# Attention of the first block: values of four heads as one feature-major product, masks on VectorE, copies on ScalarE

## What is computed

```python
def block(i):                       # 128 queries t; 8 heads of 64 in two key groups of four
    s_c = einsum("bqgrd,bkgd->bgrqk", qb, k_cmp) * scale
    p_c = masked_softmax(s_c, cmp_end[None, :] <= t[:, None])
    o_c = einsum("bgrqk,bkgd->bqgrd", p_c, v_cmp)
    ...
    s_s = einsum("bqgrd,bgqkd->bgrqk", qb, ks) * scale
    p_s = masked_softmax(s_s, causal)
    o_s = einsum("bgrqk,bgqkd->bqgrd", p_s, vs)
    ...
    s_w = einsum("bqgrd,bkgd->bgrqk", qb, kw) * scale
    p_w = masked_softmax(s_w, mask_w)
    o_w = einsum("bgrqk,bkgd->bqgrd", p_w, vw)
    o = gb[..., 0:1] * o_c + gb[..., 1:2] * o_s + gb[..., 2:3] * o_w
...
mixed = concatenate([rmsnorm(y_conv, norm_conv_out), rmsnorm(y_att, norm_attn_out)])
h = h + rmsnorm(mixed @ w_out, norm_mix_post)
mn = rmsnorm(mem, norm_mem)         # memory rows for the cross attention that follows
```

## Time and profile before

| | |
|---|---|
| median of 3 runs | 2248.43 us (2248.36 to 2249.26) |
| profiled execution, span from first to last instruction | 2246.4 us |
| its own time | not given beside the span; the median is 2.0 us above the span |
| PE busy | 2224.9 us, 99% |
| DVE, ACT, POOL busy | 1245.1 us (55%), 885.6 us (39%), 280.7 us (12%) |
| chain that ended last | PE 93%, DVE 3%, POOL 1%, ACT 1% |
| DMA | 203.19 MB, mean 90 GB/s |

### The profile page before, as it was taken

The page is one execution under the profiler, slowest core; times in us unless marked ns, Lnnn a source line. Parts: engine busy times, 40 slices in busy tenths (PEclk is TensorE's granted clock), DMA queues, the critical chain, the costliest instruction groups (busy, mean ns, idle before and its releaser), DMA issues.

```text
span 2246.4 us, 29245 instructions
## 1 busy us (share of the span) xinstructions
PE 2224.9 (99%) x11388; PEld 1821.7 (81%) x11388; DVE 1245.1 (55%) x1836; ACT 885.6 (39%) x1363; POOL 280.7 (12%) x273
## 2 busy tenths in 40 slices
PE   9999999999999999999999999999999999999999
PEld 7877888898888888886778888888887668888887
DVE  6467656445444225999664444333889664544422
ACT  5545454354333225234744333222323753433321
POOL 3000032011000001014331000001003442000000
PEclk9999999999999999999999999999999999999999
DMA  6221033122222231321122222222221112322222
GB/s 223 100 76 57 20 121 126 55 72 99 103 102 93 94 113 69 113 75 57 56 77 81 107 93 93 100 106 105 104 84 57 39 66 85 113 102 104 94 101 86
DMA packets 30484, 203.19 MB, mean 90 GB/s; under 512 B 3504, under 2 KB 4144, under 8 KB 6704
## 3 DMA queue, kind: packets, MB, share of 16 engines
q1 hardware_dynamic: 29088, 197.34, 24.4%
q10 hardware_dynamic: 1296, 4.46, 0.5%
HBM read 199.69 MB, written 2.10 MB: 90 GB/s over the span
## 4 chain that ended last, share of the span: by engine, by line
PE 93%; DVE 3%; POOL 1%; ACT 1%; issue 1%; DMA 0%; ACTq 0%; DVEq 0%; POOLq 0%
PE bank L415 26%; PE bank L417 26%; PE bank L416 26%; PE bank L2110 1%; PE bank L1002 1%; PE bank L2120 1%; PE bank L2133 1%; PE bank L973 1%; PE bank L2028 1%; POOL acc L324 1%; PE bank L990 1%; PE bank L2010 1%; PE bank L1593 1%; PE bank L1570 1%; PE bank L515 1%
## 5 line engine op out<-in xcount | busy, mean ns | idle before, releaser
L415 PE MATMUL bank<-x_hi,w_hi 128*128 128x512 f32 (+1 forms) x2032 | 789.9, 389 | 5.9 <-DVE x_lo L1766 2.3
L417 PE MATMUL bank<-x_hi,w_lo 128*128 128x512 f32 (+1 forms) x2032 | 775.0, 381 | 0.0
L416 PE MATMUL bank<-x_lo,w_hi 128*128 128x512 f32 (+1 forms) x2032 | 774.1, 381 | 0.0
L301 DVE TENSOR_TENSOR w_lo<-w_raw,w_hi 128x2048 fp32r<-128x2048 f32 x167 | 386.2, 2313 | 412.3 <-ACT w_hi L297 412.3
L297 ACT ACTIVATE w_hi<-w_raw 128x2048 fp32r<-128x2048 f32 x167 | 319.7, 1916 | 585.8 <-PE bank L417 583.9
L415 PEld LDWEIGHTS bank<-x_hi,w_hi 128*128 128x128 f32 x2032 | 382.1, 188 | 83.6 <-issue 6.8
L417 PEld LDWEIGHTS bank<-x_hi,w_lo 128*128 128x128 f32 x2032 | 381.9, 188 | 74.9
L416 PEld LDWEIGHTS bank<-x_lo,w_hi 128*128 128x128 f32 x2032 | 382.4, 188 | 72.7 <-issue 2.9
L415 PE MATMUL bank<-f_hi,w_hi 128*128 128x512 f32 (+1 forms) x572 | 213.3, 373 | 0.0
L416 PE MATMUL bank<-f_lo,w_hi 128*128 128x512 f32 (+1 forms) x572 | 213.2, 373 | 0.0
L417 PE MATMUL bank<-f_hi,w_lo 128*128 128x512 f32 (+1 forms) x572 | 213.2, 373 | 0.0
(11 more groups left out here) (355 smaller groups left out, 2637.2 us busy)
## 6 DMA issues: line engine op xcount, KB each, us to landing
w_raw<-w_d SPq DMA_DIRECT2D x184, 1024.0 KB, 4.8
out_d<-h SPq DMA_DIRECT2D x8, 256.0 KB, 6.6
h<-x_d ACTq DMA_DIRECT2D x3, 512.0 KB, 9.2
tab<-rope_d ACTq DMA_DIRECT2D x2, 640.0 KB, 3.9
memT<-mem_d ACTq DMA_DIRECT2D x1, 1024.0 KB, 4.8
w_raw<-w_d SPq DMA_DIRECT2D x2, 256.0 KB, 4.1
h<-x_d ACTq DMA_DIRECT2D x2, 256.0 KB, 5.8
w_raw<-w_d SPq DMA_DIRECT2D x1, 512.0 KB, 6.6
```

Source lines behind the costliest of these rows:

```text
L301: dve.tensor_tensor(w_lo[:, u.slot, :], w_raw[:, u.slot, :], w_hi[:, u.slot, :], ALU.subtract).then_inc(lo_ready, 1)
L415: pe.matmul(dst, wh[:, k, cols], hi[:, kx_, at:at + width], start=start, stop=False)
L416: pe.matmul(dst, wh[:, k, cols], lo[:, kx_, at:at + width], start=False, stop=False)
L417: return pe.matmul(dst, wl[:, k, cols], hi[:, kx_, at:at + width], start=False, stop=stop)
```

## The change

- A job's pair of heads is now one head of each key group (m and m + 4), so `kTx` goes; the columns of the query weights and gates and the rows of the output weights are reordered on the host. Jobs 0 to 3 of a block are the selected branch, 4 to 7 the window.
- The mask products go. DVE subtracts and masks out of PSUM into `prob` and takes the minimum in one instruction per head (`minima`); the exponential then works in place. `prob` has four buffers, so scores wait for the minimum and no longer for the exponential.
- POOL multiplies each job's probabilities by gate over sum (`job_scaled`) before they are turned; DVE does so for the compressed branch.
- The turn comes three steps after the scores; ACT copies all turned probabilities, four jobs side by side into `pT`.
- The values of four jobs are one run of products, four steps behind the last of them: 64 value columns are the weights, 512 columns (four jobs) move, and each head half writes its 64 partitions of bank 6. Both branches sum up there, and DVE adds the sum to `o_all`, now feature-major, once per block (`block_out`).
- The attention norm follows the new layout: squares summed on POOL and PE, the inverse root spread to a row, four multiplications on DVE; `mixed_turn` goes.
- The tables of the steps move, four partial output tiles (`TAIL_TILES`) stand among the last turns, and the last products and the memory rows' sums are in another order.

The core of the diff (of replaced functions the new lines; the old ones stand in the listing above):

```diff
+        J_LAG_T, J_LAG_V, C_LAG_T, C_LAG_V = 3, 4, 2, 3
+        J_STEPS = JOBS + J_LAG_V
+        J_VALUES_AT = {js[-1] + J_LAG_V: n for n, js in enumerate(J_GROUPS)}
+
+        def block_end(b_):
+
+            return 8 * b_ + 7 + J_LAG_V
...
+        GATED_AT = {**{t: 3 for t in range(-QB, 0)}, **{t: 4 for t in range(8)}, **{t: 2 for t in range(8, 16)}}
...
+        SPLIT_AT = {0: (14, 0), 1: (14, 1), 9: (15, 0), 10: (15, 1), 14: (16, 0), 15: (16, 1), 18: (17, 0), 20: (17, 1)}
+
+        CONV_AT = {6: 0, 7: 2, 8: 4, 11: 6, 12: 8, 13: 10, 16: 12, 17: 14}
+        CONV_SQ_AT = {8: (0,), 12: (1,), 14: (2,), 18: (3,)}
+        AT_CONV_SUM, AT_CONV_INV, AT_CONV_ROWS = 20, 21, 26
+        CONV_NORM_AT = {26: (0, 1), 27: (2, 3)}
+        CONV_HI_AT = {27: (0, 1), 28: (2, 3)}
+        CONV_LO_AT = {28: (0, 1), 29: (2, 3)}
+        MEM_EARLY = 2
...
-            return j // 8, j % 8 // 2, j % 2, j % 8 // 4
+            return j // 8, j % 4, j % 8 // 4
...
             def c_turn(i):
-                pe.wait_ge(j_exp, i + 1)
+                pe.wait_ge(c_w, 4 * i + 4)
...
+                for m in range(4):
+                    for e in range(2):
+                        mm = pe.matmul(bank[HD * e:HD * e + HD, 6, m * P:(m + 1) * P], vblk[:, e, m * HD:(m + 1) * HD],
+                                       pt_c[:, i % 2, e * P:(e + 1) * P], start=True, stop=True)
...
                 else:
-                    pe.wait_ge(j_exp, QB + 2 * (j - 1))
+                    pe.wait_ge(j_max, QB + 2 * (j - 1))
                 for e in range(2):
                     pe.matmul(bank[:, b_ + e, 0:n], qT[HD * e:HD * e + HD, m, i * P:(i + 1) * P],
-                              key_rows(kT, kTx, e, g)[:, br, 0:n], start=True, stop=False)
-                for e in range(2):
-                    mm = pe.matmul(bank[:, b_ + e, i * P:n], ident_b[:, :], mask_b[:, P:2 * P], start=False, stop=True)
-                mm.then_inc(j_s, 1)
+                              kT[HD * e:HD * e + HD, br, 0:n], start=True, stop=True).then_inc(j_s, 1)
...
             def turn(j):
                 i = j // 8
-                pe.wait_ge(j_exp, QB + 2 * (j + 1))
+                pe.wait_ge(j_scaled, j + 1)
                 pe.wait_ge(j_pta, QB + j)
...
+            def values(n):
+                js = J_GROUPS[n]
+                i, m0, br = job(js[0])
+                m1 = m0 + len(js)
+                pe.wait_ge(j_pta, QB + js[-1] + 1)
+                if br == 0:
+                    pe.wait_ge(j_o, QB + i)
+                for k in range(i + 1):
+                    for e in range(2):
+                        mm = pe.matmul(bank[HD * e:HD * e + HD, 6, m0 * P:m1 * P], vtok[:, k, br * P + e * HD:br * P + (e + 1) * HD],
+                                       pT[:, k, e, m0:m1, :].rearrange("p m t -> p (m t)"),
+                                       start=(br == 0 and k == 0), stop=(br == 1 and k == i))
                 mm.then_inc(j_pv, 1)
...
+            TAIL_TILES = {JOBS: (0, 0), JOBS + 1: (0, 1), JOBS + 2: (1, 0), JOBS + 3: (1, 1)}
+            for t in range(-QB, J_STEPS):
                 if t < 0:
                     c_scores(t + QB)
                 elif t < JOBS:
                     scores(t)
+                if 0 <= t + QB - C_LAG_V < QB:
+                    c_values(t + QB - C_LAG_V)
+                if t in J_VALUES_AT:
+                    values(J_VALUES_AT[t])
+                if 0 <= t + QB - C_LAG_T < QB:
+                    c_turn(t + QB - C_LAG_T)
+                if 0 <= t - J_LAG_T < JOBS:
+                    turn(t - J_LAG_T)
                 gated_chunks(GATED_AT.get(t, 0))
...
+                if t in TAIL_TILES:
...
+                    mixed_products(j, (m,), range(4))
...
             pe.wait_ge(lo_ready, U_OUT + 3)
+            pe.wait_ge(ao_added, 2 * (QB - 1))
+            column_sums(pe, bank[:, 7, 0:QB - 1], acc[:, 0:(QB - 1) * P])
+            pe.wait_ge(ao_sq, QB)
+            column_sums(pe, bank[:, 7, QB - 1:QB], *(sq[:, (QB - 1) % 2, m * P:(m + 1) * P] for m in range(4))).then_inc(ao_step, 1)
             mixed_products(2, (0,), range(4))
-            mixed_turn(0)
-            mixed_turn(1)
+            pe.wait_ge(ao_step, AO_INV)
+            spread(pe, bank[:, 6, :], small[:, 36:36 + QB]).then_inc(ao_step, 1)
             mixed_products(2, (1,), range(4))
-            mixed_turn(2)
-            mixed_turn(3)
             for k in range(4, 8):
                 pe.wait_ge(mix_lo, k + 1)
                 mm = mixed_products(0, (0, 1), (k,))
             mm.then_inc(unit_done, 1)
-            mixed_products(1, (0,), range(4, 8))
+            mixed_products(1, (0, 1), range(4, 8)).then_inc(unit_done, 1)
             stat_columns(pe, NORM_MEM, MEM)
-            mixed_products(1, (1,), range(4, 8)).then_inc(unit_done, 1)
+            mixed_products(2, (0, 1), range(4, 8)).then_inc(unit_done, 1)
             stat_rows(pe, NORM_MEM, rcol_mem)
-            mixed_products(2, (0, 1), range(4, 8)).then_inc(unit_done, 1)
             linear(pe, Unit(U_OUT + 3))
...
             def exps(j):
                 n = (j // 8 + 1) * P
+                for e in range(2):
+                    act.wait_ge(j_max, QB + 2 * j + e + 1)
+                    row = prob[:, j % 4, e, 0:n]
+                    act.activation(row, row, ACT.Exp, bias=jsm(j, 0, e), scale=-1.0, accum_out=jsm(j, 4, e)).then_inc(j_exp, 1)
+
+            def copy_turned(j):
+                i, m, br = job(j)
+                act.wait_ge(j_t, QB + j + 1)
+                if j >= 4:
+                    act.wait_ge(j_pv, QB + J_GROUP_OF[j - 4] + 1)
                 if wide(j):
+                    act.activation(pT[:, 0:i + 1, :, m, :].rearrange("p k e t -> p e k t"),
+                                   bank[:, 4:6, 0:(i + 1) * P].rearrange("p e (k t) -> p e k t", t=P), ACT.Copy).then_inc(j_pta, 1)
...
+            for t in range(-QB, JOBS + J_LAG_T):
+                if 0 <= t + QB - C_LAG_V < QB:
+                    c_out(t + QB - C_LAG_V)
+                if 0 <= t + QB - C_LAG_T < QB:
+                    c_copy(t + QB - C_LAG_T)
+                if 0 <= t - J_LAG_T < JOBS:
+                    copy_turned(t - J_LAG_T)
                 if t < 0:
                     c_e(t + QB)
                 elif t < JOBS:
...
                     exps(t)
...
+            def minima(j):
                 n = (j // 8 + 1) * P
...
+                    dve.wait_ge(j_t, QB + j - 3)
+                for e in range(2):
+                    dve.wait_ge(j_s, QB + 2 * j + e + 1)
+                    dve.tensor_tensor_reduce(prob[:, j % 4, e, 0:n], bank[:, 2 * (j % 2) + e, 0:n], causal_b[:, T - n:T],
+                                             -1.0, -LOW, ALU.add, ALU.min, jsm(j, 0, e)).then_inc(j_max, 1)
...
+            def block_out(b_):
+                o = o_all[:, :, b_ * P:(b_ + 1) * P]
+                dve.wait_ge(j_pv, QB + J_GROUP_OF[8 * b_ + 7] + 1)
+                dve.tensor_tensor(o, bank[:, 6, :].rearrange("p (m t) -> p m t", m=4), o, ALU.add).then_inc(j_o, 1)
...
             for m in range(4):
+                dve.wait_ge(ao_step, AO_ROWS)
+                dve.tensor_tensor(o_all[:, m, :], o_all[:, m, :], bank[:, 6, :], ALU.mult).then_inc(ao_n, 1)
+            for m in range(4):
                 dve.wait_ge(mix_hi, 4 + m + 1)
...
+            def job_scaled(j):
+                row = prob[:, j % 4, :, 0:(j // 8 + 1) * P]
+                pool.wait_ge(j_exp, QB + 2 * (j + 1))
+                pool.wait_ge(j_w, j + 1)
+                pool.tensor_tensor(row, row, jsm(j, 8).unsqueeze(2).to_broadcast([P, 2, (j // 8 + 1) * P]), ALU.mult).then_inc(j_scaled, 1)
...
+            for t in range(JOBS + 1):
+                if t > 0:
+                    job_scaled(t - 1)
+                for m in range(1, 4):
+                    if m in CONV_SQ_AT.get(t - 1, ()):
+                        conv_squares_added(m)
+                if 0 <= t - AT_CONV_INV - 1 < ROOT_STEPS:
+                    inverse_root(pool, t - AT_CONV_INV - 1)
+                for b_ in range(QB - 1):
+                    if t == block_end(b_) + 2:
+                        block_squares_added(b_)
```

## The result

The changed kernel took 2252.97 us (median of 12 runs, 2250.61 to 2256.12) against 2249.18 us for the kernel before beside it (12 runs, 2246.70 to 2250.66): ratio 1.0019, 95% interval 1.0011 to 1.0027. It is slower by 3.8 us: little, but the whole interval lies above 1. The prediction's range held it; its likeliest value, no change, was not what came, and the time is where the rival "slow clock" had put it (2253.4).

The account below looks back on a forecast made before the run. TensorE, busy 99% of the span, was taken as the bound. Its work -19.1, old waits -3.3, new waits +12.2, +0.8, +1.9 and +5.7, and clock +1.7 gave -0.1 us: 2248.3 us, range 2237 to 2256.

Parts of the forecast that it names:

- slow clock: Rival, chance 0.20: in steps 16 to 31 each idle slot brings a low-clock stretch, three uncounted costing 5.1 us: 2253.4 us.
- TensorE's own work: First block: old values, masks and row turns removed, new values and small work added on TensorE: -19.1 us.
- that rival: Rival, chance 0.03: in the new values the head halves take turns, 2.1 us a key tile, +22 us, 2270.
- Waits: First block: old waits go (-3.3), new in wide steps (+12.2), blocks 0 and 1 (+0.8), tail (+1.9), memory rows (+5.7).
- the surest term: Memory rows' sums moved: the fourth output unit waits 6.8 us for its weights' remainder, +5.7 us.
- Steps 16 to 31: Steps of blocks 2 and 3, without weight chunks: other engines need 53.2 us against TensorE's 41, +12.2 us of waits.
- the turn of job 29: In the tail, this turn waits 1.2 us for copy 28, part of the tail's +1.9 us.
- ACT's queue sets the pace instead: Steps 16 to 31: ACT's copies, exponentials, idle slots and extra operations come to 48.2 us against TensorE's 41.
- The rule on sharing the reading of PSUM: All copies go to ACT against this rule: with it binding the wide steps have their 12.2 us waits, without it none.
- The clock: Two 1.2 GHz stretches, behind the 6.8 us wait and in the wide steps, one more than before: +1.7 us.
- The prediction's own signs: Right if first product on attention rows starts about 7.5 us earlier; wrong if more than two low stretches come.
- dense values keep columns flowing: Argument against the rival "slow clock": in steps 16 to 31 the dense value products keep TensorE's columns flowing.

Follow-up runs that it names:

- run 1: Changed kernel with the memory rows' sums and row spread back in the order of the kernel before: 2246.55 us, ratio 0.9992 to the kernel before.
- Run 7: run 1 plus three order changes: POOL's root rounds ahead of scaling, two units split earlier, one row tile rounded per step; 2241.01 us.
- run 6: run 1 plus wide jobs' copies split, ACT copying bank 4 and DVE bank 5: 2251.63 us.
- run 8: run 1 with POOL multiplying only two columns of each head's probabilities, leaving out gate over sum: 2238.34 us.
- run 9: Run 7 plus unit 17's half splits and the convolution's last square and sum later, two root rounds in one step: 2240.03 us.
- run 10: Run 7 plus 19 idle products of ones in five TensorE waits of steps 20, 29, 30 and 32: 2238.34 us.
- run 2: Changed kernel plus 50 idle products of ones in TensorE's wait ahead of the fourth output unit: 2256.19 us.
- run 5: run 1 plus 33 idle products of ones in eight TensorE waits of steps 17 to 32: 2244.77 us.
- run 3: Changed kernel plus 71 idle products of ones in eight TensorE waits of steps 17 to 32: 2253.62 us.
- run 4: Changed kernel with filler chunk, half split and convolution tables as in the kernel before, convolution rows two steps later: 2253.57 us.

## Why the prediction was right and wrong

The sum forecast -0.1 us, and the profiled executions differ by +5.2 (the medians by 3.8). Term by term, from these two executions:

- **TensorE's own work: forecast -19.1, measured -18.1. Right.** From 118 us to the fourth unit the kernel before takes 179.7 us, less 4.4 idle and 1.7 of low clock: 173.6. The changed one takes 181.1, less 19.9 and 5.7: 155.5. A key tile costs 0.93 us (1.87 for two) against 1.0, so the halves do run in pairs, and that rival fell.
- **Waits: forecast +17.3 (-3.3 + 12.2 + 0.8 + 1.9 + 5.7), measured 19.9 - 4.4 = +15.5. Right in size.** The memory rows, "the surest term", wait 6.55 us against 6.8, and run 1 shows that their place alone makes it. Steps 16 to 31 hold 10.6 us against 12.2 (of the 11.8, the turn of job 29 belongs to step 32, where it waits 1.21 as forecast).
- **But the waits' cause was half wrong.** The step read "ACT's queue sets the pace instead", with 7.2 us on ACT and 5.0 on DVE and POOL. Measured are 3.4 on ACT (4.6 less step 32's) and 7.0 on DVE (2.3) and POOL (4.7). Run 7 took most of the latter away by order alone; run 6 shows that relief for ACT's copies on DVE makes it worse. In the sum I added DVE's and POOL's delays from rows without the two side by side; beside POOL the remainder of a row tile on DVE takes twice as long (run 8). A minimum of 384 columns, put at 0.67 us, took 0.55.
- The rule on sharing the reading of PSUM between ScalarE and VectorE, from "TensorEngine Tiling (Array Packing)" of the Trainium skill, section Performance Considerations, did not help here: in run 6 the sharing cost 5.1 us, at the one place in DVE's queue that was tried.
- **The clock: forecast +1.7, measured +7.3. This is the step that failed.** It said "I expect two: behind the 6.8 us wait and once in the wide steps". Five stretches came, two of them twice as long, 23.9 us in all. They cost 9.0 us, and less the 1.7 of before (an upper bound) that is 5.6 more than forecast; the misses of the other terms (+1.0, -1.8, and 0.5 from ahead of 118 us) nearly cancel: -18.1 + 15.5 + 7.3 + 0.5 = +5.2. The prediction's own signs say the same: more than two low stretches came, and the first product on attention rows started 3.6 us earlier than before instead of 7.5.
- **The rival "slow clock" had the mechanism, and its time, within 0.4 us, is partly luck.** It counted five stretches of 3.4 us, four of them in the idle slots of the steps. Five came, but three in the steps and two from the fourth unit on, as long as seven of 3.4; a part of them lay over waits, where a low clock costs nothing. The price of 1.7 us for 3.4 us of work is about right (1.2 to 1.7): from the fourth unit to the end the profiled executions take 1948.6 to 1949.0 us without a low stretch (before, runs 6 and 8 to 10) and 1950.2 to 1950.3 with one of 3.4 us (runs 2, 5 and 7). The argument against it, "dense values keep columns flowing", is refuted by step 19, whose values ran at 1.2 GHz from end to end.
- **What brings the low clock is shown in part.** With the same waits filled or half filled, the clock stayed at 1.00 in the profiled steps of runs 3 and 5 and at the fourth unit of run 2, and the clocks of whole executions rose from run to run (0.994 to 0.997 against 0.997 and 0.998 in run 3; 0.995 to 0.998 against 0.997 to 1.000 in run 5). But waits do not bring it each time: run 9's profiled execution has 9.2 us of them in the steps at 1.00. And the stretch at 320.46 came in run 2 without a wait for 30 us ahead of it, so its part of the 9.0 us (1.2 to 1.7) cannot be put down to idle time.
- "TensorE: Matmul & The Clock Gate" of the Trainium skill, section "A second HAM failure mode", describes short idles of TensorE between groups of products that make its clock go up and down. The waits of 1.06, 1.40 and 1.22 us around 197.6 us agree with it; run 9's, of up to 1.7 us, left the clock at 1.00.

What I did not test: the mask in DVE's minimum alone, and a second set of buffers for the turned probabilities.

## What to carry to other kernels

When work is taken off TensorE and the other engines then set the pace, price the idle time twice: as time, and as the clock that it can take down for the work that follows; count the second as a chance, since executions of one kernel differ in it. Look in the queues of the other engines for what stands ahead of the chain, and move that before moving the work itself; here three changes of order gave 5.5 us. Where a wait must stay, idle products that are shorter than the wait, priced from a row of the same form, raised the clock and gave 1.8 us on top of run 1; the 2.7 on top of run 7 are not clear of chance.

## What was not expected

- DVE beside POOL: remainders from SBUF took 1550 ns instead of 750, a minimum out of PSUM did not change (685 and 687). "SBUF — State Buffer" of the Trainium skill, section "Who interferes with whom", says that DVE and GpSimd share a pair of SBUF ports which one of them holds at a time; the rows agree.
- A stretch at 1.2 GHz some 8 us into the products on the memory rows came in the profiles of the changed kernel and of runs 1 to 5 and 7, with TensorE busy for some 19 us or more ahead of it, and not in those of the kernel before and of runs 6 and 8 to 10. In each it began during 24 records of products with four moving columns (in the changed kernel from 318.18 to 321.08 us), or up to 0.4 us behind them. The executions without the stretch have the same records, so they alone do not bring it; what does is open.
